# First attention of a two-layer decoder kernel: the first decode pair is computed inside the last two projection units

## What is computed

```python
qkv = h @ w_qkv                                  # 12 projection units of 256 columns
q, k = rope(rms_norm(q, g_q), pos), rope(rms_norm(k, g_k), pos)
k_all, v_all = concat([past_k, k]), concat([past_v, v])    # decode: 1024 + 16 keys
for each query block:                            # 8 heads, two maps (c = 0, 1) each
    p = softmax(mask(q . k * scale))
    w = p[c=0] - lam * p[c=1]
    o = w @ v
o = rms_norm(o, g_sub) * (1 - lam_init)
x = x + o @ w_o                                  # unit group "oa"
x = x + swiglu(rms_norm(x))                      # then layer two
```

## Time and profile before

| what | value |
|---|---|
| median of 3 runs (lowest, highest) | 1642.45 us (1639.75, 1643.95) |
| the profiled execution: its time, its span | 1639.72 us, 1637.9 us |
| granted TensorE clock | 1.000 of full speed throughout |
| PE, DVE, ACT, POOL busy, share of the span | 99%, 69%, 44%, 9% |
| HBM read, written | 249.79 MB, 15.73 MB |

### The profile page before, as it was taken

The page is one execution under the profiler, slowest core; times in us unless marked ns, Lnnn a source line. Parts: engine busy times, 40 slices in busy tenths (PEclk is TensorE's granted clock), DMA queues, the critical chain, the costliest instruction groups (busy, mean ns, idle before and its releaser), DMA issues.

```text
span 1637.9 us, 31443 instructions
## 1 busy us (share of the span) xinstructions
PE 1616.6 (99%) x13180; PEld 1486.7 (91%) x13180; DVE 1132.0 (69%) x1576; ACT 722.5 (44%) x1196; POOL 151.9 (9%) x132
## 2 busy tenths in 40 slices
PE   9999999999999999999999999999999999999999
PEld 8888766699999999999999897766999999999999
DVE  5765477678984797488742337877689748964874
ACT  6444476765551344134432214666555413531441
POOL 0000000012210011011000100000122101110110
PEclk9999999999999999999999999999999999999999
DMA  7133899931222122222243458997422221221222
GB/s 288 64 113 139 348 420 419 419 151 52 87 95 104 52 78 103 78 69 87 103 150 136 168 210 350 419 419 325 167 78 78 104 78 55 101 104 52 78 104 90
DMA packets 40252, 267.54 MB, mean 163 GB/s; under 512 B 4400, under 2 KB 4784, under 8 KB 10928
## 3 DMA queue, kind: packets, MB, share of 16 engines
q1 hardware_dynamic: 36720, 252.95, 40.2%
q0 software_dynamic: 3392, 12.58, 2.2%
HBM read 249.79 MB, written 15.73 MB: 162 GB/s over the span
## 4 chain that ended last, share of the span: by engine, by line
PE 86%; DMA 5%; DVE 5%; issue 2%; ACT 2%; SPq 0%; DVEq 0%; ACTq 0%
PE ps L584 30%; PE ps L799 29%; PE ps L268 4%; PE ps L270 4%; PE ps L269 4%; DMA kv<-in_v_s 3%; PE ps L1264 2%; PE ps L1323 2%; DVE s_lo L748 2%; PE ps L1205 2%; PE ps L611 2%; PE ps L1242 1%; DMA kv<-in_v_a 1%; DMA xT<-in_v_a 1%; PE ps L1227 1%
## 5 line engine op out<-in xcount | busy, mean ns | idle before, releaser
L230 ACT ACTIVATE w_hi<-w_raw 128x2048 fp32r<-128x2048 f32 x55 | 105.0, 1909 | 189.8 <-PE ps L584 158.5
L246 DVE TENSOR_TENSOR w_lo<-w_raw,w_hi 128x2048 fp32r<-128x2048 f32 x55 | 126.0, 2292 | 71.7 <-ACT w_hi L230 71.7
L744 ACT ACTIVATE s_hi<-t 128x512 fp32r<-128x512 f32 x176 | 109.4, 626 | 144.5 <-PE ps L799 65.5
L799 PE MATMUL ps<-hs_hi,s_hi 128*128 128x320 f32 x528 | 163.8, 310 | 0.0
L799 PE MATMUL ps<-hs_lo,s_hi 128*128 128x320 f32 x528 | 163.2, 309 | 0.0
L799 PE MATMUL ps<-hs_hi,s_lo 128*128 128x320 f32 x528 | 163.2, 309 | 0.0
L584 PE MATMUL ps<-gu_hi,w_hi 128*128 128x320 f32 x692 | 157.8, 309 | 0.2
L584 PE MATMUL ps<-gu_lo,w_hi 128*128 128x320 f32 x692 | 157.7, 309 | 0.0
L584 PE MATMUL ps<-gu_hi,w_lo 128*128 128x320 f32 x692 | 157.7, 309 | 0.0
L748 DVE TENSOR_TENSOR s_lo<-t,s_hi 128x512 fp32r<-128x512 f32 x176 | 133.0, 762 | 5.3 <-ACT s_hi L744 4.5
L657 DVE TENSOR_TENSOR sg<-ps,rows 128x640 f32<-128x640 f32 x47 | 38.7, 823 | 128.5 <-PE ps L584 128.5
(11 more groups left out here) (302 smaller groups left out, 3968.2 us busy)
## 6 DMA issues: line engine op xcount, KB each, us to landing
w_raw<-in_w SPq DMA_DIRECT2D x99, 1024.0 KB, 4.8
kv<-in_k_a SPq DMA_DIRECT2D x12, 1024.0 KB, 17.7
kv<-in_v_a SPq DMA_DIRECT2D x12, 1024.0 KB, 18.0
kv<-in_v_s SPq DMA_DIRECT2D x12, 1024.0 KB, 17.0
kv<-in_k_s SPq DMA_DIRECT2D x12, 1024.0 KB, 20.3
xT<-in_k_a SPq DMA_DIRECT2D x8, 1024.0 KB, 18.6
xT<-in_k_s SPq DMA_DIRECT2D x8, 1024.0 KB, 13.7
work<-in_v_a SPq DMA_DIRECT2D x7, 1024.0 KB, 16.5
```

Source lines behind the costliest of these rows:

```text
L230: nc.scalar.activation(w_hi[s][:, :, :], w_raw[:, s, :, :], ACT.Copy).then_inc(hi_done, 1)
L246: nc.vector.tensor_tensor(w_lo[s][:, :, :], w_raw[:, s, :, :], w_hi[s][:, :, :].bitcast(F32), ALU.subtract).then_inc(lo_done, 1)
L744: nc.scalar.activation(s_hi[i][:, :, :], factor(j % 2, i), ACT.Copy).then_inc(hi_done, 1)
L799: last = nc.tensor.matmul(ps[:, bank[i], 0:HALF], w[:, p, :], m[:, p, :], start=(i < 3 and p == 0 and a == 0), stop=(p == 3 and a == 2), s ...
```

## The change

- `stage`, `rot` and `swp` move from `work` into `v5`, whose columns are not written before units 8 to 11 are copied out. So two ring places in `work` are free as soon as the first norm is summed. The values of units 8 and 9 overwrite `rot` and `swp` and now wait for the four key stores.
- `RING_A` is reordered, and SP issues five pieces (k0, k1, half of v0) before the fifth weight unit instead of three. The first weight unit of "oa" follows the last "qkv" unit directly. Then come v0's second half, k2 (into x0 and x1), v1 (`w_hi0`, `w_lo0`), k3, v2 (`w_hi1`, `w_lo1`).
- PE does in unit 10 the scores of pair 0 (behind t = 0) and its transposes (behind t = 3), in unit 11 its values (t = 0), prompt step 0's scores (t = 1), and prompt step 1's and pair 1's scores (t = 3). Unit 9's transposes move inside unit 9 (t = 2).
- Pair 0 uses other places: its weights in `rows`, turned weights in banks 5 to 7, its output in bank 7, queries `qs` in the last tiles of x.
- Slots 0 and 1 of all three engines are written out in a new order. In slot 15 the split of the first "oa" unit on ACT is cut in halves, the second behind `act_w1`.
- The reload of the residual also waits until the scores of the last pair are done.

```diff
 def quarter(n):
-    return work[:, 2 * n:2 * n + 2, :].rearrange("p a n -> p (a n)").rearrange("p (t c) -> p t c", t=TT)
-stage = work[:, 0:4, :].rearrange("p a n -> p (a n)").rearrange("p (t c) -> p t c", t=TT)
-rot, swp = quarter(2), quarter(3)
+    return v5[:, :, n * UC:(n + 1) * UC]
+stage = v5[:, :, 2 * UC:4 * UC]
+rot, swp = quarter(0), quarter(1)
...
+            def pe_early(self, unit, t):
+                step = (unit, t)
+                if step == (10, 0):
+                    self.pe_s(0)
+                elif step == (10, 3):
+                    self.pe_w1(0)
+                    self.pe_w2(0)
+                    self.pe_wn(0)
+                elif step == (11, 0):
+                    self.pe_v(0)
+                elif step == (11, 1):
+                    self.pe_ps(0)
+                elif step == (11, 3):
+                    self.pe_ps(1)
+                    self.pe_s(1)
...
             def pe_a(self, pe):
-                for n in range(N_PAIRS):
+                self.pe_ps(2)
+                self.pe_pt(0, 0)
+                self.pe_w1(1)
+                self.pe_pt(1, 0)
+                self.pe_w2(1)
+                self.pe_pv(0)
+                self.pe_ps(3)
+                self.pe_pt(2, 0)
+                self.pe_wn(1)
+                self.pe_o(0)
+                self.pe_pv(1)
+                self.pe_pv(2)
+                self.pe_ps(4)
+                self.pe_s(2)
+                self.pe_v(1)
+                for n in range(2, N_PAIRS):
...
             def act_a(self, act, begin, first, stored):
...
+                self.act_sx(1)
+                self.act_pt(0, 0)
+                self.act_px(2)
+                self.act_w1(1)
+                self.act_pt(1, 0)
+                self.act_px(3)
+                self.act_pt(2, 0)
+                self.act_px(4)
+                self.act_sx(2)
+                for n in range(2, N_PAIRS):
...
-                            split_hi(act, first, 0, 0)
+                        split_hi_half(act, first, 0)
...
                     self.act_w1(n)
+                    if n + 1 == N_PAIRS:
+                        split_hi_half(act, first, 1)
...
 # ACT, projection
                 else:
+                    qk_tevac(act, b)
+                    act.wait_ge(qk["stored"], 64)
                     token_evac(act, "qkv", m, lambda t: v5[:, t, 0:2 * UC], qk["ev"])
-                qk_tevac(act, b)
             split_hi(act, "qkv", 11, 1)
+            ta.act_sx(0)
+            ta.act_w1(0)
             act.wait_ge(mm, tiles_before("qkv", 11))
             token_evac(act, "qkv", 5, lambda t: v5[:, t, 2 * UC:4 * UC], qk["ev"],
-                       lambda t: ta.act_px(0) if t == 0 else ta.act_sx(0) if t == 2 else None)
+                       lambda t: ta.act_osb(0) if t == 2 else ta.act_px(0) if t == 3 else ta.act_px(1) if t == 4 else None)
...
 # SP
-            ta.loads(sp_, slice(0, 3), {r: [(norm["lo"], KT), (norm["sq"], KT)] for r in ("x0", "x1")})
+            x_free = [(norm["lo"], KT), (norm["sq"], KT)]
+            ta.loads(sp_, slice(0, 5), {"x0": x_free, "x1": x_free, "work0": [(norm["sum"], KT - 1)]})
             load_units(4, u_a)
-            ta.loads(sp_, slice(3, 5), {"work0": [(qk["stored"], 64), (qk["tr"], 8)]})
             load(u_a, 0)
```

More of the change, by code:

```diff
@@ L1117, in bank, with early, weights, out @@
                 return B_PS if n == 0 else 0
+            def early(self, n):
+                return n == 0 and not self.b
+            def weights(self, n):
+                return rows[:, :, :].rearrange("p a c -> p (a c)") if self.early(n) else self.sp[n % G]
+            def out(self, n):
+                return ps[:, B_PV, P:2 * P] if self.early(n) else ps[:, B_O, 0:P]
+            def turned_new(self, n):
+                return ps[:, B_PV if self.early(n) else B_N, WN_C:WN_C + P]
             def z(self, n):
@@ L1200, in pe_ps @@
                 self.wait(pe, s["pu" if self.b else "px"], k)
-                if k == 1:
+                if k == 1 and self.b:
                     pe.wait_ge(s["x"], 1)
+                if k == 0 and not self.b:
+                    pe.wait_ge(s["wev"], 1)
+                    pe.wait_ge(s["wne"], 1)
                 for c in range(2):
@@ L1233, in pe_pv @@
                 self.copied(pe, self.rounds(k + 1))
+                if k == 0 and not self.b:
+                    pe.wait_ge(s["oev"], 1)
                 if i == 0:
@@ L1255, in pe_s @@
                     self.wait(pe, s["x"], n)
-                if n == 0:
-                    pe.wait_ge(s["pu" if self.b else "px"], 1)
+                if n == 0 and self.b:
+                    pe.wait_ge(s["pu"], 1)
+                if n == 1 and not self.b:
+                    pe.wait_ge(qk["ev"], 6 * TT - 2)
                 for h in part:
@@ L1322, in pe_v @@
                         for t in range(4):
-                            last = nc.tensor.matmul(ps[self.rows(t), B_O, 0:P], swt[g][:, 4 * h + k, self.rows(t)],
+                            last = nc.tensor.matmul(out[self.rows(t), :], swt[g][:, 4 * h + k, self.rows(t)],
                                                     vh[:, k, t * P:(t + 1) * P], start=h == 0 and k == 0, stop=False,
@@ L1330, in pe_v @@
                 for t in range(4):
-                    last = nc.tensor.matmul(ps[self.rows(t), B_O, 0:P], swn[:, g, self.rows(t)],
+                    last = nc.tensor.matmul(out[self.rows(t), :], swn[:, g, self.rows(t)],
                                             v5[:, QB, g * 512 + t * P:g * 512 + (t + 1) * P], start=False, stop=True,
@@ L1471, in act_w1 @@
                 nc.scalar.wait_ge(s["w1"], n + 1)
-                nc.scalar.activation(swt[n % G][:, 0:4, :].rearrange("p k c -> p (k c)"), ps[:, 0, :], ACT.Copy)\
+                nc.scalar.activation(swt[n % G][:, 0:4, :].rearrange("p k c -> p (k c)"),
+                                     ps[:, B_PS if self.early(n) else 0, :], ACT.Copy)\
                     .then_inc(s["wev"], 1)
```

132 lines of the change are left out of this document (78 added, 54 removed).

## The result

The changed kernel took 1644.99 us in the median of 22 executions (1641.29 to 1646.79), the kernel before 1642.04 us in as many beside it (1639.69 to 1645.44): ratio 1.0017, 95% interval 1.001 to 1.0023. The forecast was 1643.5 us. The profiled execution has a span of 1642.7 us against 1637.9 us. These two are not alike: that of before (1639.72 us) is within 0.03 us of the fastest of its 22, that of after (1644.54 us) is 0.45 us under its median. So two us or so of what the profiles differ by is a matter of which execution was profiled.

What follows compares the result with a forecast made beforehand. Late first-attention slots were held bound by the cache stream at full DMA rate, restarted at unit 11's end. DMA +0.7 and slot 15 +0.4 gave +1.1 us, put on the 1642.45 us median: 1643.5 us, range 1639.5 to 1648.

Steps and rivals of the forecast that it cites:

- The end of unit 11: PE work moved into units 10 and 11 makes unit 11 end 5.7 us later (5.6 to 6.0), at 190.2 us.
- Pieces loaded at the restart: Cache stream, first attention: 12 pieces instead of 10 issued before unit 11 ends, 4.97 us less; DMA term +0.7 us.
- The ledger: Model of the first attention's end: cache pieces left after the stream restarts at unit 11's end, 2.48 us each.
- earns nothing: Loading two pieces in the first 30 us instead of at 154.65 us gains nothing beyond the two fewer pieces.
- Slots 0 and 1: First attention: new order's stalls put slot 2 at 203 to 204.5 us, 2 to 3 us late, at no cost.
- the 5.76 us of slack: PE's six waits for transfers in the first attention's late slots, said to take up the delay of the early slots.
- Slot 15: End of the first attention: halving the first w_o split delays the sub-norm's logarithm, +0.4 us (0 to +0.7).
- All after "oa" shifted by the same amount: Everything behind the start of "oa" at 336.3 us was to be later by the same 1.1 us.
- The late key store: Slower rival: the last key store lands late, delaying copies and unit 10; up to 4.7 us, 1648.2 us; chance 0.07.
- The ring was not starved: Slower rival: early slots cost PE 8 us, the stream stops again, +4 us more, 1647.5 us; chance 0.06.
- The restart did hold the stream: Faster rival claimed the opposite: unit 11's end is no gate, two pieces are clear gain, 1637.9 us; chance 0.04.
- PE has the last word: Rival: PE's own chain, not DMA, sets the first attention's end if over 5.76 + 0.7 us longer; nearly same time.

Runs made afterwards that it cites:

- late_loads: The changed kernel with its two early loads (k1's second half, v0's first half) issued behind the weight units again: 1644.83 us, 1.0015 of before.
- act_reorder: The changed kernel with ACT's copy for step 2 (slot 1's transposed weights) issued ahead of step 3's exponential: 1644.06 us, 1.0019 of before.
- whole_split: The changed kernel with slot 15's split of the first w_o unit in one piece again: 1643.58 us, 1.0011 of before.
- base_again: The kernel before the change, unchanged, run for a second profile: 1641.22 us, 0.9995 of before.
- half_pieces_b: The changed kernel loading only half of each second-attention cache piece from the seventh on, products running over old data in the rest: 1636.17 us, 0.9967 of before.
- pair1_early_w12: pair1_early with 12 warm-up products instead of 20 at PE's start: 1641.72 us, 1.0002 of before.
- scores_back: The changed kernel with prompt step 1's row products and pair 1's scores moved out of unit 11 to slot 0's head: 1645.41 us, 1.0020 of before.
- pair1_early: The changed kernel with pair 1's scores at unit 11's first step, four more pieces under way, ACT and DVE reorderings, split in one piece: 1639.98 us, 0.9992 of before.
- back_reorder: scores_back with ACT's copy for step 2 ahead of step 3's exponential and slot 15's split in one piece: 1642.02 us, 1.0008 of before.
- pe_shift: The changed kernel with 52 warm-up products of 64 columns at PE's start instead of 20 of 128: 1660.67 us, 1.0119 of before.

## Why the prediction was right, and where it was not

**The end of unit 11: right mechanism, term too small.** Predicted +5.7 us (5.6 to 6.0); measured 190.85 against 184.53, +6.3 us. The moved work itself measured 5.75 us (2.65 + 2.20 + 0.90) against my 5.64. The three breaks, priced at up to 0.1 us each, measured 0.1 us each, but only 0.06 us of them are in the 5.7. Of the rest, 0.27 us, both traces have 0.15 already at the last key store (146.78 us against 146.63); what is left is noise.

**Pieces loaded at the restart: right.** 6.32 us later, two pieces of 2.48 us fewer: 6.32 - 4.97 = +1.35 us. v14's half moved by +1.42 us. The ledger holds; the predicted +0.7 was the unit's end again. late_loads bears out "earns nothing".

**Slots 0 and 1: right, the margin thinner than said.** Slot 2 at 204.60 us, in the upper edge of 203 to 204.5, the copy behind step 3's exponential as the main stall (2.27 us of the predicted 2.5). It is hidden: act_reorder halves it, slot 2 begins 1.46 us earlier, and "oa" gains 0.37 us. Of the 5.76 us of slack 2.85 are left in the waits for transfers. The prediction counted the stalls as the only user of it; the "issue" wait of 0.78 us in slot 12, up to 1.40 us in other kernels, and the clock that fell behind the 2.27 us stall in five of six traces were not foreseen.

**Slot 15: right sign, +0.6 instead of +0.4 us** (bounds 0 and +0.7), by whole_split.

**All after "oa" shifted by the same amount: wrong for the profiled executions.** "oa" itself is later by 2.01 us where 1.1 was forecast. Behind it the second attention added 2.5 us in the profile: PE's instruction packets came late at other products, and for longer. The prediction had no term for that. In the medians about 0.9 us are left for it (2.95 us less 2.01), and with the interval of 1.6 to 3.8 us this may also be nothing. How much of the 2.5 us is the change's is not shown: after, late_loads, whole_split and act_reorder have one PE program, and B of 173.62, 173.44, 171.27 and 171.15 us. The stream has a bound of its own there: the three executions that wait for transfers at the end of the second attention and have no long "issue" wait behind them (before, base_again, act_reorder) show 171.1 to 171.4 us, where PE alone would take some 165 (half_pieces_b).

**The number.** 1643.5 us was forecast, 1644.99 measured: 0.9 us of it is "oa", 0.9 us the second attention, and -0.4 us the kernel before, whose median of 22 is 1642.04 and not 1642.45 us.

**The rivals.** The late key store did not hold: unit 10 was not delayed. The ring was not starved. The restart did hold the stream: the ledger's +1.35 us came true, and pair1_early_w12, which feeds it from other free places, has v14's second half 3.45 us sooner behind the end of unit 11. "PE has the last word" was given no chance of its own; it is false for the change as made, with 0.46 to 1.40 us to spare, and true for scores_back, whose stream is 2.8 us earlier. The late wait alone does not prove the bound; that act_reorder makes PE 1.46 us earlier and "oa" only 0.37 does.

**What stays open.** What decides in an execution whether an instruction block or a cache piece is the late one was not settled, so neither is the share of the second attention in the 3 us. That pair1_early stays at 175.3 to 176 us under three placements has two reasons in sight, slowest executions and a clock that falls behind its long waits (once or twice in each trace), and no run that parts them. Nor is it known why the clock did not fall in after.

## What to carry to other kernels

When a prefetch stream is held by a gate, a ledger of pieces (how many are in before the gate, how late the gate opens, how long one takes) gives the end to a tenth of a microsecond; price the gate's delay completely, the breaks in the run of products too. (In pair1_early_w12, where the places changed too, two pieces brought 3.45 and not 4.97 us.) Before moving work to help one of two nearly equal bounds, work out where the other one stands: moving pair 1's scores back freed the stream and ran into PE, and only the kernel that shortened both brought "oa" forward, by 2.4 us. In a kernel whose DMA engines are full for a long time, keep some microseconds for PE's instructions arriving late: any edit that adds or removes PE instructions moves those waits, also in parts it does not touch. And where executions of one kernel are 4 to 5 us apart, see where in that spread the profiled one lies before laying a difference of 2 us between two profiles to an edit.

## What the runs showed of the hardware that was not expected

- PE waits of 0.2 to 2.5 us at multiples of 256 PE instructions (248 without the semaphore instructions), each ending 1.2 to 1.6 us after an instruction packet has landed. In after all six lie in the two attentions, behind stretches with a DMA share of 0.93 to 1.02; at 0.50 to 0.81 in the second attention there is none (half_pieces_b).
- The same stall of 2.27 us was followed by a fall of the granted clock to its lower level in five traces (scores_back: 0.72 over 6 us) and not in after (1.00 over 197 to 203 us). In the second attention a wait of 2.48 us was followed by 0.79 over 8 us in pair1_early, waits of 2.14 us in after and 2.46 in back_reorder were not. A stall of 1.15 us or less at that place in slot 1 was followed by none (act_reorder, back_reorder and the three kernels of pair1_early).
- 104 warm-up products of 64 columns took 22.45 us, 0.22 us each, more than the 0.15 us each of 40 products of 128 columns. The traces show the clock in it: in after the first 13 stand 0.21 to 0.23 us apart too and the rest, from 3.9 us on, 0.11; in pe_shift all 104 stand 0.21 us apart, and the first unit's products 0.43 us apart up to 26.4 us, 0.23 after it. The trace's records of the full clock begin at 3.93 and 26.44 us. Why the clock rose so much later in pe_shift was not tried.
